# A two-block transformer kernel: one plain block fewer in each feed-forward, one seven-product block more

## The reference

```python
def swiglu_ffn(h, w_in, w_out):
    gate, up = jnp.split(h @ w_in, 2, axis=-1)
    return (jax.nn.silu(gate) * up) @ w_out

def swiglu(h, w_gate, w_up, w_down):
    return (jax.nn.silu(h @ w_gate) * (h @ w_up)) @ w_down
```

## Time and profile before

| what | value |
|---|---|
| median of the runs | 2367.5 us |
| profiled execution, its time | 2370.04 us |
| profiled execution, span | 2368.2 us |
| PE (matmul) busy | 2339.0 us, 99% |
| DVE busy | 1624.6 us, 69% |
| ACT busy | 1227.5 us, 52% |
| POOL busy | 263.5 us, 11% |
| mean granted clock of TensorE | 0.997 of full |

### The profile page before, as it was taken

One profiled execution on the slowest core, in us unless ns is written; L12 is line 12 of the kernel. 1 busy time (PEld: TensorE's weight loads), 2 busy tenths in 40 slices (PEclk: granted clock), 3 DMA queues, 4 the chain that ended last, 5 costly groups with the idle time before them and its releaser, 6 DMA issues.

```text
span 2368.2 us, 35242 instructions
## 1 busy us (share of the span) xinstructions
PE 2339.0 (99%) x14096; PEld 2006.6 (85%) x14096; DVE 1624.6 (69%) x2333; ACT 1227.5 (52%) x1998; POOL 263.5 (11%) x210
## 2 busy tenths in 40 slices
PE   8999999999999999999999999999999999999998
PEld 7777778776788888899989899988887888899997
DVE  5688745478775355687786788785677565787784
ACT  7766654355564254445554555553644354555542
POOL 0000000455200010110002200001032201100002
PEclk9999999999999999999999999999999999999999
DMA  6221234333575332343233233223322232333222
GB/s 199 79 72 51 84 107 156 107 103 107 175 225 205 104 119 63 90 125 108 90 98 107 81 121 104 83 95 107 115 64 63 89 115 72 104 111 103 91 75 90
DMA packets 177269, 251.97 MB, mean 106 GB/s; under 512 B 9936, under 2 KB 101328, under 8 KB 177104
## 3 DMA queue, kind: packets, MB, share of 16 engines
q1 hardware_dynamic: 175952, 248.13, 33.4%
q10 hardware_dynamic: 1152, 1.57, 0.2%
HBM read 231.83 MB, written 16.78 MB: 105 GB/s over the span
## 4 chain that ended last, share of the span: by engine, by line
PE 94%; DVE 3%; ACT 1%; issue 0%; DMA 0%; POOL 0%; SPq 0%; DVEq 0%; POOLq 0%; ACTq 0%
PE bank L1473 92%; PE bank L1633 1%; DVE wlo L2468 1%; PE bank L1656 0%; DVE T L2476 0%; PE bank L1754 0%; PE bank L1778 0%; DMA zb<-scr_z 0%; ACT whi L1872 0%; DVE W L2468 0%; DMA raw<-in_w_in 0%; PE bank L1599 0%; POOL xw L3368 0%; DVE xg L2472 0%; ACT E L2124 0%
## 5 line engine op out<-in xcount | busy, mean ns | idle before, releaser
L1473 PE MATMUL bank<-xopr,shi 128*128 128x256 f32 x3360 | 605.0, 283 | 0.0
L1473 PEld LDWEIGHTS bank<-xopr,shi 128*128 128x128 f32 x3360 | 524.5, 192 | 0.5
L1473 PE MATMUL bank<-xopr,slo 128*128 128x256 f32 x1680 | 475.4, 283 | 0.0
L2468 DVE TENSOR_TENSOR wlo<-raw,whi 128x1024 fp32r<-128x1024 f32 (+2 forms) x286 | 352.5, 1236 | 130.5 <-ACT whi L1872 130.1
L1473 PE MATMUL bank<-xh,whi 128*128 128x512 f32 x1016 | 411.5, 405 | 8.5 <-DVE wlo L2468 8.5
L1473 PE MATMUL bank<-xh,wlo 128*128 128x512 f32 x1016 | 397.9, 392 | 0.0
L1473 PE MATMUL bank<-xl,whi 128*128 128x512 f32 x1016 | 397.2, 391 | 0.0
L1872 ACT ACTIVATE whi<-raw 128x1024 fp32r<-128x1024 f32 (+2 forms) x286 | 292.9, 1031 | 144.8 <-PE bank L1473 129.2
L1473 PEld LDWEIGHTS bank<-xopr,slo 128*128 128x128 f32 x1680 | 322.5, 192 | 0.0
L1473 PEld LDWEIGHTS bank<-xh,whi 128*128 128x128 f32 x1016 | 191.5, 188 | 64.9 <-issue 20.2
L1473 PEld LDWEIGHTS bank<-xh,wlo 128*128 128x128 f32 x1016 | 191.3, 188 | 41.7
(11 more groups left out here) (390 smaller groups left out, 4288.7 us busy)
## 6 DMA issues: line engine op xcount, KB each, us to landing
raw<-in_w_in SPq DMA_DIRECT2D x92, 512.0 KB, 3.7
quarter<-in_w_ffn_in SPq DMA_DIRECT2D x32, 512.0 KB, 4.5
quarter<-in_ffn_gate SPq DMA_DIRECT2D x32, 512.0 KB, 3.9
quarter<-in_ffn_up SPq DMA_DIRECT2D x32, 512.0 KB, 4.9
raw<-in_ffn_down SPq DMA_DIRECT2D x28, 512.0 KB, 4.4
raw<-in_w_xattn_kv SPq DMA_DIRECT2D x16, 512.0 KB, 4.1
raw<-in_w_kv_mem SPq DMA_DIRECT2D x16, 512.0 KB, 4.6
raw<-in_w_branch_ssd SPq DMA_DIRECT2D x16, 512.0 KB, 4.4
```

The costliest lines, as they stand in the source:

```text
L1473: return e.matmul(out, l, r, start=start, stop=stop, skip_group_check=skip)
L2468: return e.tensor_tensor(out, a, b, op)
```

## The change

PLAIN goes from 3 to 2, so each feed-forward has two plain blocks and nine seven-product ones. The first such block is now number 2; its quarters get two tiles of their own at 146 and 154 KB, where the hidden tiles of blocks 7 to 10 come later. They are loaded as soon as all engines have passed the mark at the start of the feed-forward and SP comes to them. `operands` has rate 4.5 in place of 3, since there are 32 tiles m in place of 48 beside which its steps can be put.

```diff
-        quarter = [at_kb(kb, [P, 2, 4, 256], name="quarter") for kb in (0, 8, 72, 80)]
+        quarter = [at_kb(kb, [P, 2, 4, 256], name="quarter") for kb in (0, 8, 72, 80, 146, 154)]
...
-        PLAIN = 3
+        PLAIN = 2
...
-            return e if i % 2 else 2 + e
+            return 4 + e if i == PLAIN else e if i % 2 else 2 + e
...
-                built.append(start(operands(tag), 3))
+                built.append(start(operands(tag), 4.5))
...
                 elif before:
                     for event in quarter_done(tag, *before[-1]):
                         w.wait_ge(*event)
+                elif r > 3:
+                    for other in ("pe", "act", "dve", "pool"):
+                        w.wait_ge(*at(other, tag))
                 elif r > 1:
                     w.wait_ge(*at("w used", ids[2 * r - 3]))
```

## The result

The changed kernel takes 2399.7 us (median of 4 runs, 2398.6 to 2400.9) beside 2367.9 for the kernel before on the same chip (2367.3 to 2370.2): a ratio of 1.0131, 95% interval 1.0119 to 1.0143, or +31.8 us. The forecast was 2392.9, range 2374 to 2405. So direction and mechanism came out, and the size was some 6 to 7 us short (31.8 against +25.4 by the differences); the question for the experiments is which terms were too small, and whether those that fit do so for the stated reason.

The account below looks back on a forecast made before the run. TensorE, busy 99% of the span, was taken to bound the kernel, with VectorE the resource to watch. The terms -4.5 + 22.4 + 0 + 4.0 + 3.5 = +25.4 us put the median at 2392.9 us, range 2374 to 2405.

Parts of the forecast that it names:

- Part 1: TensorE's work: one plain block (21.69 us) becomes a seven-product one (20.19) in each of three feed-forwards, -4.5 us in all.
- Part 2: Product operands: VectorE finishes them late, so TensorE waits 7.7 us in "fa" and "fc", 7.0 in "fb", +22.4 us.
- The layout of VectorE's work by hand: VectorE's steps from R to the first product, waits included: TensorE due at 1010.1 waits to about 1016.8, 6.7 us.
- The second wait, before product (2,5): TensorE waits again for lo part 1 of pair 3, 9 matmuls later: about 1.0 us in "fa", 0.3 in "fb".
- no idle time: Lower bound on the operand holes: VectorE's 28.7 us of queued work without idle moments, ending at 1010.3; 2 us each.
- B: Rival: VectorE uses its idle time and closes within the last tiles, no hole opens, 2363 us; chance 0.06.
- C: Rival: steps overlap better than laid out, holes of only 2 to 3 us, 2368 to 2380 us; chance 0.13.
- Part 3: First pair's quarters at 146 and 154 KB: their loads are hidden under block 1, 0 us.
- Part 4: Raw-ring shift, 96 to 99 slots per feed-forward: delays seed_f before the down-projection's last product in "fb" and "fc", +4.0 us.
- Part 5: TensorE's clock at half behind the new holes: +1.0, +1.5, +1.0, together +3.5 us; bounds 0 and 10.
- rival D: Clock stays at half over two or more stretches behind each hole and the bank-copy wait: 2403 to 2412 us; chance 0.08.
- Sum: All terms over the whole kernel: +25.4 us, 2392.9 us on the median of the runs.

Follow-up runs that it names:

- the edits alone: Kernel before, three plain blocks kept, with the first pair's quarters at 146 and 154 KB and operand steps at rate 4.5: 2368.9 us, ratio 1.0001.

## Why the prediction was right, and by how much it missed

- **Part 1 (-4.5).** The sign holds and the size roughly: 2.5 to 4.5 us by the account above.
- **Part 2 (holes, forecast 22.4, measured 23.5).** The mechanism is right; that the sum came so close is in part luck. The layout of VectorE's work by hand for "fa" has the right order, its idle gaps too: sum 3 beside GpSimd from 1010.34 (laid out as ending 1013.7; it ended 1012.9), lo part 0 of pair 3 released TensorE at 1016.6 (forecast 1016.8). But this execution ran 1.0 us ahead (R is copied at 978.47, 979.49), so from R on VectorE took 0.8 us longer than laid out: the last low part was stretched by 1.06 beside GpSimd, where the layout had allowed 0.5 at most. "fa" 7.24 against 6.7 + 1.0, "fc" the same, "fb" 9.00 against 7.0. Two errors met. The second wait, before product (2,5), did not come: at half clock the matmuls ahead of it came 0.216 us apart (25 of them in 5.39 us of the window behind the hole) instead of 0.120, and the operand was there first. But in the kernel with useless matmuls and the clock whole it was 0.34 us, so the forecast 1.0 was too long in either case. In "fb" the order was misread: the forecast put one slo behind the last low part, and the trace has both ahead of it (1360.94 and 1365.61), and a weight sum and an up product besides, which in "fa" stand behind it (1.14 + 0.60 us):

```profile
1365.61 1.70 DVE L2468 TENSOR_TENSOR slo<-wsum,shi 128x1024 fp32r<-128x1024 f32 x1
1367.23 2.66 DVE L2468 TENSOR_TENSOR xop<-xop 128x512 f32<-128x512 f32 x3
1369.81 1.22 DVE L2468 TENSOR_TENSOR wsum<-wsum,quarter 128x1024 f32<-128x1024 f32 x1
1370.95 0.68 DVE L2468 TENSOR_TENSOR four<-bank,T 128x512 f32<-128x512 f32 x1
1371.55 0.95 DVE L2468 TENSOR_TENSOR xopr<-xop,xopr 128x768 fp32r<-128x768 f32 x1
```

  Its norm 0, sum 3 and slo were stretched as well (2.37, 2.66 and 1.70 us), and its first low part waited 0.71 for ScalarE, itself held by a copy of R that waited 1.76 for GpSimd; how much of the 2 us each of these is was not measured. The bound "no idle time" (2 us a hole) was far off, and so were rivals B and C that rested on it.
- **Part 3 (0).** Right: no wait of TensorE on a quarter's load, and the edits alone cost nothing.
- **Part 4 (+4.0).** The count of slots was right in all three places (none in "fa", 1.84 and 1.9 in "fb" and "fc": 3.7). But undoing it gave back 6.1 us: I had priced the wait and not the clock behind it, although its length was in part 5's own rows. In the kernel before the shift's two waits were followed by half clock only once.
- **Part 5 (+3.5, measured 7 to 11).** This is the term that was mis-sized. The step that failed was "each 3.4 us at half rate ... loses up to 1.7": I took one such stretch behind a hole and let a second wait absorb part of it. The trace shows 10.2 us at half around each hole, of which 4.3 to 5.3 hold dense matmuls, and one more stretch behind each bank wait: 10.9 us by half of TensorE's busy time in them, 9.1 by what is over when waits and swap (-4.5) are taken off, and 7.3 by the kernel with useless matmuls (5.6 less, with one stretch of 1.7 left). The Trainium skill, page "TensorE: Matmul & The Clock Gate", section "HAM oscillation — how this bites in real kernels", puts the loss at half of the throttled time; the rows agree at most for the part that holds matmuls, and for no other. This was rival D's mechanism ("half over two or more stretches"), at a smaller price than D gave it.
- **Sum.** -4.5 + 23.5 + 0 + 3.7 + 10.9 = +33.6 by terms (30.0 with the 7.3), +31.8 by the medians, against +25.4. The profiled execution of after reached the first gate of "fa" 1.1 us earlier than that of before (982.5, 983.6); that lies ahead of the change, and I don't explain it.

## What to carry to other kernels

Before you drop a block of dense matmuls in front of a phase that needs prepared operands, lay out the preparing engine's queue between the earliest input and the new need, in the order of issue, with each measured wait and each neighbour that slows it; a sum of busy times is a lower bound: here it gave 28.7 us, where the trace shows 36.0 (980.58 to 1016.55). Price a hole in TensorE as its length plus what the lower clock takes from the matmuls behind it; the second goes if TensorE is kept at work, both if the order of the steps closes the hole. If a change alters how many slots a cyclic buffer has used, count the residues of every later phase: here that alone cost 6 to 7 us.

## What the runs showed of the hardware

- In the feed-forwards, around a single wait of TensorE of 7 to 9 us the granted clock was at half for 10.2 us in most cases (once 6.8), around 4 to 7 us for 6.8, around 2.8 to 3.4 us for 3.4 (6.8 where a wait of 1.0 us came behind it), around 1.8 to 2.4 us for 3.4 in 11 of 13 cases, and around 1.0 to 1.7 us never. The prediction had put no half clock behind the bank waits of 2 us.
- Matmuls of no use, 8 to 10 of 512 columns in float32, kept the clock whole where a wait of 7 to 9 us had halved it: 7.0 us of them (8.9 in "fb") in place of each wait, some 3.5 to 5.5 us gained over the three.
- GpSimd's 512-column multiplication, 1.5 us on its own engine, cost VectorE 1.0 us, and VectorE does the same work in 0.68: in this window handing it over made the engine that gave it away later, not earlier; in the kernel before, where no product waits for an operand, the move changed nothing (2369.4 against 2368.6).
